# Parts of units between turns back and forth, and each root behind its turn back, at the seam of output projection and feed-forward network

## What is computed

```python
    h = h + hybrid_mixer(...)          # ends in: einsum('bld,de->ble', y, w_out)
    u = rms_norm(h, norm_ffn)          # h * rsqrt(mean(h*h) + eps) * gain
    hid = einsum('bld,df->blf', u, w_up)   # then convolution, silu, gate
    h = h + einsum('blf,fd->bld', silu(gate) * val, w_down)
```

## Time and profile before

| | us |
|---|---|
| median of 3 runs (1705.42 to 1706.94) | 1705.45 |
| the profiled execution's own time | 1707.96 |
| its span, from the first instruction to the last | 1706.1 |
| TensorE matmul busy | 1669.5 (98%) |
| VectorE busy | 893.7 (52%) |
| ScalarE busy | 600.7 (35%) |
| GpSimd busy | 494.6 (29%) |

### The profile page before, as it was taken

How to read it: one execution, slowest core, us unless ns; L and a number is a source line. 1 busy time by engine, 2 the same in 40 slices (tenths; PEclk the granted TensorE clock), 3 DMA queues, 4 the chain that set the end, 5 groups by cost and what they waited for, 6 DMA issues and landing times.

```text
span 1706.1 us, 30483 instructions
## 1 busy us (share of the span) xinstructions
PE 1669.5 (98%) x12103; PEld 1598.7 (94%) x12103; DVE 893.7 (52%) x970; ACT 600.7 (35%) x982; POOL 494.6 (29%) x472
## 2 busy tenths in 40 slices
PE   7999999999999999999899999999999999999997
PEld 6999999999999999999899999998998998989986
DVE  5556455575444454554443654644545545455447
ACT  6334455444343343443423431222222212212214
POOL 3212212247345433444211122122122211221210
PEclk9999999999999999999999999999999999999999
DMA  5223443259546445455872021111111111211112
GB/s 183 69 91 103 132 141 98 80 153 210 145 123 169 125 136 147 122 147 143 222 264 66 25 63 50 37 57 41 49 37 51 52 44 37 61 49 37 49 37 99
DMA packets 242512, 168.24 MB, mean 99 GB/s; under 512 B 43913, under 2 KB 228840, under 8 KB 241306
## 3 DMA queue, kind: packets, MB, share of 16 engines
q1 hardware_dynamic: 209494, 135.30, 28.1%
q10 hardware_dynamic: 32740, 32.08, 5.6%
q0 software_dynamic: 224, 0.12, 0.0%
HBM read 125.10 MB, written 42.37 MB: 98 GB/s over the span
## 4 chain that ended last, share of the span: by engine, by line
PE 93%; DVE 3%; DMA 1%; ACT 1%; issue 1%; DVEq 0%; POOL 0%; ACTq 0%; SPq 0%
PE gb L906 68%; PE db L1253 11%; PE db L1050 4%; PE mb L1253 2%; PE db L964 1%; PE db L1121 1%; PE db L1120 1%; DVE cacc L1765 1%; DMA yo<-ot_d 1%; DVE fino L2188 0%; PE db L1047 0%; PE db L1193 0%; PE db L1203 0%; DMA yb_d<-ybs 0%; PE db L918 0%
## 5 line engine op out<-in xcount | busy, mean ns | idle before, releaser
L906 PE MATMUL gb<-u_hi,w_hi 128*128 128x342 f32 (+2 forms) x2520 | 820.4, 326 | 11.7 <-DVE u_lo L2056 6.9
L906 PE MATMUL gb<-u_lo,w_hi 128*128 128x342 f32 (+2 forms) x2520 | 808.2, 321 | 0.0
L906 PE MATMUL gb<-u_hi,w_lo 128*128 128x342 f32 (+2 forms) x2520 | 805.1, 319 | 0.0
L781 POOL TENSOR_TENSOR w_lo<-w_raw,w_hi 128x1024 fp32r<-128x1024 f32 x130 | 328.2, 2528 | 1037.8 <-ACT w_hi L1297 1037.4
L906 PEld LDWEIGHTS gb<-u_hi,w_hi 128*128 128x128 f32 x2520 | 476.1, 189 | 16.0 <-issue 12.5
L906 PEld LDWEIGHTS gb<-u_lo,w_hi 128*128 128x128 f32 x2520 | 476.3, 189 | 0.4
L906 PEld LDWEIGHTS gb<-u_hi,w_lo 128*128 128x128 f32 x2520 | 475.9, 189 | 0.0
L1297 ACT ACTIVATE w_hi<-w_raw 128x1024 fp32r<-128x1024 f32 x130 | 135.6, 1051 | 7.1 <-ACT tm L1396 5.2
L1765 DVE SCALAR_TENSOR_TENSOR cacc<-xb,prm,cacc 128x1040 f32<-128x1040 f32 x72 | 124.6, 1731 | 10.5 <-issue 8.4
L2153 DVE TENSOR_TENSOR h<-h,db 128x512 f32<-128x512 f32 x138 | 92.5, 684 | 42.2 <-PE db L1253 41.8
L1664 ACT ACTIVATE a_hi<-cv 128x1024 fp32r<-128x1024 f32 x21 | 22.3, 1060 | 248.8 <-PE db L1253 200.5
(11 more groups left out here) (264 smaller groups left out, 1814.7 us busy)
## 6 DMA issues: line engine op xcount, KB each, us to landing
w_raw<-in_w_in SPq DMA_DIRECT2D x53, 512.0 KB, 4.2
w_raw<-in_w_up SPq DMA_DIRECT2D x44, 512.0 KB, 3.8
w_raw<-in_w_down SPq DMA_DIRECT2D x22, 512.0 KB, 3.4
qkT_d<-sl ACTq DMA_DIRECT2D x16, 576.0 KB, 2.8
kv_d<-tm ACTq DMA_DIRECT2D x16, 576.0 KB, 3.4
tk<-kv_d SPq DMA_DIRECT2D x9, 1024.0 KB, 7.7
w_raw<-in_w_out SPq DMA_DIRECT2D x11, 512.0 KB, 8.5
kT<-qkT_d SPq DMA_DIRECT2D x9, 512.0 KB, 5.2
```

The source lines that it names most:

```text
L781: pool.tensor_tensor(lo, w_raw[:, n % SLOTS, :], hi.bitcast(F32), ALU.subtract).then_inc(s_wlo, 1)
L906: mm = pe.matmul(gb[:, bank, 0:w], wt, u, start=(k == 0 and m == 0), stop=(k == KT - 1 and m == 2))
```

## The change

From ("unit", 2, 2) to ("up", 1, 0), five units are cut into parts of some of their 8 steps, and the turns are put between the parts. Only the first part waits, and only the last one signals. On ScalarE, root2(j) stands behind back(j) for every tile, where it stood behind forth(j-1), that is after high2(j-1). VectorE's loop is as it was.

```diff
-for _j, _unit in enumerate([("unit", 7, 1), ("unit", 2, 2), ("unit", 6, 2), ("unit", 7, 2), ("up", 0, 0),
-                            ("up", 1, 0), ("up", 0, 1)]):
-    OUT_PLAN += [_unit, ("back", _j + 2), ("forth", _j + 1)]
-OUT_PLAN += [("up", 1, 1), ("forth", KT), ("up", 0, 2), ("up", 1, 2)]
+OUT_PLAN += [("unit", 7, 1), ("back", 2), ("forth", 1)]
+def parts(kind, n, b, *cuts):
+    edges = (0,) + cuts + (KT,)
+    return [(kind, n, b, k0, k1) for k0, k1 in zip(edges, edges[1:])]
+_a, _b, _c = (parts("unit", n, 2, *cuts) for n, cuts in ((2, (3, 6)), (6, (1, 4, 7)), (7, (2,))))
+_d, _e = parts("up", 0, 0, 2, 5), parts("up", 1, 0, 1, 4)
+OUT_PLAN += [_a[0], ("back", 3), _a[1], ("forth", 2), _a[2], _b[0], ("back", 4), _b[1], ("forth", 3),
+             _b[2], ("back", 5), _b[3], _c[0], ("forth", 4), _c[1], _d[0], ("back", 6), ("forth", 5),
+             _d[1], ("back", 7), _d[2], _e[0], ("forth", 6), _e[1], ("back", 8), _e[2], ("forth", 7),
+             ("up", 0, 1), ("forth", KT), ("up", 1, 1), ("up", 0, 2), ("up", 1, 2)]
...
@@ tensor
-                    n, b = tile
+                    n, b, k0, k1 = span(*tile)
...
-                    w_ready(k)
-                    pe.wait_ge(s_gfree, U_OUT - 3 + q + 1)
+                    if k0 == 0:
+                        w_ready(k)
+                        pe.wait_ge(s_gfree, U_OUT - 3 + q + 1)
...
+                    else:
+                        mm = unit(k, q % 3, o, w, k0, k1)
+                    if k1 == KT:
+                        mm.then_inc(s_g, 1)
+                        q += 1
...
@@ scalar
                 elif kind == "back":
-                    if tile[0] < 2:
-                        root2(tile[0])
+                    root2(tile[0])
                 else:
                     high2(tile[0])
-                    if 0 < tile[0] < KT:
-                        root2(tile[0] + 1)
```

More of the change, by code:

```diff
@@ L150 @@
 OUT_PLAN += [("unit", 2, 1), ("back", 0), ("unit", 6, 1), ("back", 1), ("forth", 0)]
-for _j, _unit in enumerate([("unit", 7, 1), ("unit", 2, 2), ("unit", 6, 2), ("unit", 7, 2), ("up", 0, 0),
-                            ("up", 1, 0), ("up", 0, 1)]):
-    OUT_PLAN += [_unit, ("back", _j + 2), ("forth", _j + 1)]
-OUT_PLAN += [("up", 1, 1), ("forth", KT), ("up", 0, 2), ("up", 1, 2)]
-OUT_UNITS = [s[1:] for s in OUT_PLAN if s[0] == "unit"]
+OUT_PLAN += [("unit", 7, 1), ("back", 2), ("forth", 1)]
[8 more added lines that the diff above has]
+             ("up", 0, 1), ("forth", KT), ("up", 1, 1), ("up", 0, 2), ("up", 1, 2)]
+OUT_UNITS = [s[1:3] for s in OUT_PLAN if s[0] == "unit" and (len(s) == 3 or s[4] == KT)]
 assert sorted(OUT_UNITS) == [(n, b) for n in range(KT) for b in range(3)]
@@ L454, in second, with span @@
             return isinstance(n, int) and n == 1
+        def span(n, b, k0=0, k1=KT):
+            return n, b, k0, k1
         def gain(row, n=KT):
@@ L1209, in _ @@
                 if kind == "unit":
-                    n, b = tile
+                    n, b, k0, k1 = span(*tile)
                     o, w = OBLOCKS[b]
                     k = W_OUT + out_slot(n, b)
-                    w_ready(k)
-                    pe.wait_ge(s_gfree, U_OUT - 3 + q + 1)
-                    for hf in range(2):
-                        if (n, b) in FIRST_OF_BLOCK:
-                            pe.wait_ge(s_y, 2 * b + hf + 1)
-                        mm = unit(k, q % 3, o, w, 4 * hf, 4 * hf + 4)
-                    mm.then_inc(s_g, 1)
-                    q += 1
+                    if k0 == 0:
+                        w_ready(k)
+                        pe.wait_ge(s_gfree, U_OUT - 3 + q + 1)
+                    if (n, b) in FIRST_OF_BLOCK:
+                        for hf in range(2):
+                            pe.wait_ge(s_y, 2 * b + hf + 1)
+                            mm = unit(k, q % 3, o, w, 4 * hf, 4 * hf + 4)
+                    else:
[3 more added lines that the diff above has]
+                        q += 1
                 elif kind == "OT":
@@ L1223, in _ @@
                 elif kind == "up":
-                    n, b = tile
+                    n, b, k0, k1 = span(*tile)
                     o, w = OBLOCKS[b]
[L1226 to L1230, removed]
+                    if k0 == 0:
+                        w_ready(W_UP0 + n)
+                        pe.wait_ge(s_u2, 2 * NORMED[b])
+                        pe.wait_ge(s_gfree, U_OUT - 3 + q + 1)
+                    mm = unit(W_UP0 + n, q % 3, o, w, k0, k1)
+                    if k1 == KT:
+                        mm.then_inc(s_g, 1)
+                        q += 1
                 elif kind == "back":
@@ L1619, in _ @@
                 elif kind == "unit":
-                    n, b = tile
+                    n, b, k0, k1 = span(*tile)
+                    if k1 < KT:
+                        continue
                     o, w = OBLOCKS[b]
```

## The result

The changed kernel took 1712.47 us (median of 9 runs, 1710.73 to 1716.26), the kernel before 1706.17 us (median of 9 runs on the same chips). The ratio is 1.0039, with a 95% interval of 1.0030 to 1.0048: slower by 0.39%, where +0.39% was forecast.

What follows compares the result with a forecast made beforehand. TensorE bound the kernel before; the change makes a ScalarE-VectorE loop of 6.02 us per tile the bound. 3.8 us won and about 10.5 lost give 6.7 us: 1705.45 + 6.7 = 1712.1 us, range 1709.5 to 1715.0.

Steps and rivals of the forecast that it cites:

- The waits that go: TensorE ahead of ("up", 0, 1) and ("up", 0, 2): about 1.85 us each, plus 0.1 at forth(8), 3.8 us won.
- a loop of 4.3 to 4.8 us: Old order, high2 ahead of root2: 4.3 us per tile, some 4.8 where high2 held up the root.
- the closed loop: ScalarE and VectorE: residual, root2, high2, low2, scale2, next residual; 6.02 us per tile against TensorE's 4.9.
- about 10.5 us lost: TensorE waits of 0.8 to 1.8 us ahead of each forth from 2 to 8 and ahead of back(6).
- The cuts cost nothing: Changes between matmuls and transposes at 10 more places: taken as 0, bounds 0 and 0.8 us.
- Its start: First round, tile 2: scale2(2) ends at 931.90, with back(2) at 925.10; TensorE waits 1.45 us for it.
- The extras: Added to six rounds: copy and w_high of (6, 2) 1.31 us, two up-projection copies 0.36 each, w_low 0.3.
- the collision: scale2(5) on VectorE beside GpSimd's moved w_low: 3.66 against 3.36 us, 0.3 us added.
- Carried whole to the end: Behind ("up", 0, 2) both kernels run the same list, so the whole 6.7 us delay reaches the end.
- The rival of the clock: TensorE falls to 1.2 GHz after idleness: some 20 us more, 1732 us; chance 0.02.

Runs made afterwards that it cites:

- Experiment 1: Changed kernel with root2 put back behind high2 and the unit cuts kept; 1702.17 us against 1705.10 for the kernel before, ratio 0.9981.
- (5): Changed kernel with the w_high between root2(5) and high2(4) moved behind the copy of (7, 2); ratio to the kernel before 1.0031.
- Experiment 2: Kernel before with only root2 moved behind its back, no unit cut; ratio to the kernel before 1.0043.

## Why the prediction was right

- **The waits that go.** Worth 3.8 us by the sum. Experiment 1 gave 3.06. Most of the rest is the ring of that kernel: forth(2), (3) and (4) are 4.79 us apart (929.07, 933.86, 938.65), over the 4.56 us of work that TensorE has between them. The forecast had named a loop of 4.3 to 4.8 us for this order, but TensorE's work was counted with an average of 4.9 and not round by round; that was the step that was rough. The forecast time does not rest on it: the 6.7 us were worked out along the closed loop to forth(8), and the "about 10.5 us lost" are only 6.7 + 3.8. Measured against experiment 1, they are 9.45.
- **The cuts cost nothing.** Shown by the pieces of experiment 1.
- **The closed loop.** Forecast 6.02 us, measured 5.98. Three edits tried it: taking high2 off the root (1), putting VectorE's list in the same order (3), shortening the root (4). With the last two, the distance of the turns forth was what the loop then adds up to, 5.5 and 4.8 us. With the first it was 4.8 as well, but by another ring, through TensorE; without high2 and low2 the old one adds up to 4.3. The lengths of residual, low2 and scaling were not changed by themselves.
- **Its start.** scale2(2) was to end 6.80 us after back(2) begins; it ended after 6.77 (929.75 - 922.98).
- **The extras.** 1.31, 0.36, 0.36 and 0.3 us were added to 36.1. The rounds measured 7.58, 6.32 and 6.33 against 5.98, so 1.60, 0.34 and 0.35. The first holds the w_high and the collision (5). forth(8) came 45.00 us after back(2), where 45.3 was forecast; the 0.3 us are six times the 0.04 of a round, and hundredths at the ends.
- **Carried whole to the end.** 6.4 us in the seam, 6.7 us by the ratio (0.0039 of 1706.17, with an interval of 5.1 to 8.2), 6.3 us between the medians. From ScalarE's copy of ("up", 1, 2) to the end of the span it is 729.95 us before (1706.1 - 976.15) and 729.98 after (1710.4 - 980.42), so no later stage took any of it back. That 1712.1 is within 0.4 us of 1712.47 is in part luck: the sum was 0.3 us too high, and it started from a median of 1705.45, which in nine runs is 1706.17.
- **The rival of the clock** did not come in the change: its waits of up to 1.5 us left the granted clock at 1.00 from 921 to 985 us. Experiment 2 shows that it was nearer than its 0.02 suggests, and that its size there was 1.5 us per fall, not 20. The forecast's ground, that waits of under 2 us should leave the clock alone, did not hold there: its second fall came behind waits of 1.15 and 1.62 us.

That ScalarE does not run high2 past a root that waits is what the traces with the new order show: by the estimate above, high2(3) could have started some 0.5 us before the waiting root did, and it came behind it. The Trainium skill, "TensorE: Matmul & The Clock Gate", section "Architectural detail", has this queue as strictly in order, and the traces agree. The Trainium skill's "GPSIMD Engine Reference", section "1. Specifications", has scale2 exposed to GpSimd's use of the shared interface; 1.60 us against 1.28 agrees.

## What to carry to other kernels

When each engine walks its own list, write the waits of two lists down side by side and look for a ring: a step that waits for the other engine with the step that the other one needs queued behind it. The length of the ring is the least time per tile, however idle both engines are. "Start it as early as possible" put the root ahead of high2, whose input was there first, on an engine that takes its list in order; cutting units, so that TensorE has work between one turn and the next, was good by itself and was hidden by that. When one ring is opened, look for the next: in experiment 1 it ran through TensorE. And compare TensorE's work with the ring round by round, not on average.

## What the runs showed of the hardware

- In experiment 2, TensorE's clock fell to 1.2 GHz behind 3.49 us of idleness, and again where TensorE had been busy 1.53 of 4.00 us although the last pause was only 1.62 us. The kernel before has that same pause of 1.62 us twice, between stretches of full work, and kept 2.4 GHz (granted clock 1.00 from 953 to 957 and from 965 to 969 us). A fall cost 1.5 us. There, waits that came close together cost more than their length; one trace shows it, and what sets the fall off was not tried.
- Between VectorE's scaling and GpSimd's w_low, the one that began later was the one that grew. In the changed kernel w_low, begun within scale2(3), took 3.15 us where it takes 2.40 in experiment 1 beside a residual, while that scaling kept its 1.28. The other way round, scale2(5), begun within a w_low of 2.39 us, took 1.60 and ended 1.09 us after it.

```profile
934.83 3.15 POOL L796 TENSOR_TENSOR w_lo<-w_raw,w_hi 128x1024 fp32r<-128x1024 f32 x1 [29.62 <-ACT w_hi L1319]
```
